# A decoder layer's input projection by Strassen's scheme, with its weight sums on VectorE and GpSimd

## The reference

```python
z = jnp.einsum("bsd,de->bse", h, w_in) + b_in
glu_val, glu_gate, gate_c, q, k, v, f_logit, gate_a = _split_columns(z)
y_conv = _conformer_conv(glu_val, glu_gate, w_dw, b_dw, g_cn, b_cn)
y_conv = y_conv * jax.nn.silu(gate_c)
y_attn = _forgetting_attention(q, k, v, f_logit)
y_attn = y_attn * jax.nn.silu(gate_a)
y = jnp.concatenate([y_conv, y_attn], axis=-1)
sub = jnp.einsum("bse,ed->bsd", y, w_out) + b_out
h = _layer_norm(DN_ALPHA * h + sub, g_post, b_post)
```

## Time and profile before

| what | value |
|---|---|
| median of 3 runs | 1765.31 us (1764.43 to 1766.93) |
| span of the profiled execution | 1763.0 us |
| TensorE busy | 1733.5 us (98%) |
| VectorE busy | 1071.8 us (61%) |
| ScalarE busy | 539.6 us (31%) |
| GpSimd busy | 215.4 us (12%) |
| transfers | 178.09 MB, 101 GB/s over the span |

### The profile page before, as it was taken

The page is one execution under the profiler, slowest core; times in us unless marked ns, Lnnn a source line. Parts: engine busy times, 40 slices in busy tenths (PEclk is TensorE's granted clock), DMA queues, the critical chain, the costliest instruction groups (busy, mean ns, idle before and its releaser), DMA issues. The chain is left out here.

```text
span 1763.0 us, 21898 instructions
## 1 busy us (share of the span) xinstructions
PE 1733.5 (98%) x7644; PEld 1400.0 (79%) x7644; DVE 1071.8 (61%) x1669; ACT 539.6 (31%) x791; POOL 215.4 (12%) x176
## 2 busy tenths in 40 slices
PE   7999999999999999999999999999999999999997
PEld 5888888888888888888888888888688877788885
DVE  4356757667586575765857657577754565344347
ACT  4323223222232232223223232232544432222240
POOL 0120101201012010110111101100200044000000
PEclk8999999999999999999999999999999999999999
DMA  5333342333323433333333333333233333332232
GB/s 157 109 110 87 95 110 71 110 97 94 100 73 108 105 91 96 77 104 110 95 92 77 108 100 95 98 83 86 70 108 96 119 131 132 124 115 95 95 120 96
DMA packets 259691, 178.09 MB, mean 101 GB/s; under 512 B 8193, under 2 KB 246945, under 8 KB 258737
## 3 DMA queue, kind: packets, MB, share of 16 engines
q1 hardware_dynamic: 258656, 170.39, 33.6%
q0 software_dynamic: 1008, 7.34, 1.2%
HBM read 173.48 MB, written 4.23 MB: 101 GB/s over the span
## 5 line engine op out<-in xcount | busy, mean ns | idle before, releaser
L635 PE MATMUL ps<-xh,wh 128*128 128x512 f32 x1792 | 716.4, 400 | 0.7 <-DVE wl L876 0.7
L636 PE MATMUL ps<-xl,wh 128*128 128x512 f32 x1792 | 711.9, 397 | 0.0
L637 PE MATMUL ps<-xh,wl 128*128 128x512 f32 x1792 | 711.5, 397 | 0.0
L876 DVE TENSOR_TENSOR wl<-raw,wh 128x1024 fp32r<-128x1024 f32 x280 | 370.3, 1324 | 391.0 <-ACT wh L388 387.1
L635 PEld LDWEIGHTS ps<-xh,wh 128*128 128x128 f32 x1792 | 338.8, 189 | 81.5 <-DVE wl L876 0.8
L637 PEld LDWEIGHTS ps<-xh,wl 128*128 128x128 f32 x1792 | 338.4, 189 | 81.8
L636 PEld LDWEIGHTS ps<-xl,wh 128*128 128x128 f32 x1792 | 338.9, 189 | 80.1 <-issue 0.5
L388 ACT ACTIVATE wh<-raw 128x1024 fp32r<-128x1024 f32 x280 | 288.2, 1054 | 297.0 <-PE ps L637 221.8
L921 DVE SCALAR_TENSOR_TENSOR y<-u,taps,y 128x512 f32 (+1 forms) x240 | 193.6, 807 | 0.0
L921 DVE SCALAR_TENSOR_TENSOR odd<-u,taps,odd 128x512 f32<-128x512 f32 x224 | 186.6, 833 | 0.0
L635 PE MATMUL ps<-wh,yh 128*128 128x512 f32 x464 | 183.0, 394 | 3.1 <-DVE yl L1162 3.1
(11 more groups left out here) (167 smaller groups left out, 1068.3 us busy)
## 6 DMA issues: line engine op xcount, KB each, us to landing
raw<-in_w_in_dram SPq DMA_DIRECT2D x224, 512.0 KB, 3.7
raw<-in_w_out_dram SPq DMA_DIRECT2D x64, 512.0 KB, 3.6
probs<-forget_sums_dram SPq DMA_DIRECT2D x16, 256.0 KB, 7.4
res<-in_x_dram POOLq DMA_DIRECT2D x4, 1024.0 KB, 5.3
out_dram<-res SPq DMA_DIRECT2D x8, 512.0 KB, 2.7
probs<-forget_sums_dram SPq DMA_DIRECT2D x16, 192.0 KB, 6.2
probs<-forget_sums_dram SPq DMA_DIRECT2D x16, 128.0 KB, 4.8
y<-in_x_dram SPq DMA_DIRECT2D x2, 768.0 KB, 9.0
```

Of the source, the lines that this page charges most:

```text
L635: nc.tensor.matmul(o, ah, bh, start=start, stop=False, skip_group_check=True)
L636: nc.tensor.matmul(o, ah, bl, start=False, stop=False, skip_group_check=True)
L637: return nc.tensor.matmul(o, al, bh, start=False, stop=True, skip_group_check=True)
L876: vec.tensor_tensor(wl[:, 2 * par + h, :], raw[:, h, :], wh[:, 2 * par + h, :], ALU.subtract) \
```

## The change

The input projection is made by Strassen's scheme (Winograd's form) over blocks of two by two. A *group* g is two tiles of weights (128 columns each) by the two halves of the 2048 rows, and its four blocks (B11, B12, B22, B21; 1024 rows by 128 columns each, 512 KB) are loaded into a ring of seven slots in `raw`. The tokens are the other two halves (256 each). In place of eight block products there are seven, called units, each of 8 x 3 matmuls of 128 by 128 by 256. There are 56 groups (48 for the heads, then 8 for `gate_c`) and 392 units.

- Four sums of weight blocks a group: `sum_1` and `sum_2` on VectorE, `sum_3` and `sum_4` on GpSimd, each of 128 by 1024, in `raw`. The sums of the input's blocks are made once at the start (`x_sums`), and the input is kept as seven factors (`xh`, `xl` of 7 x 8 x 256).
- Each unit has its own weights to split: 392 `high` and `low` of 1024 columns (224 before).
- Products are added up in PSUM where the scheme allows it, and otherwise by small instructions: three copies on ScalarE (`p1`, `p5`, `nu1`) and five on VectorE (`c12`, `c22`, `c21`, `c11`, `s57`) a group, all of 256 columns.
- The seven factors of the input take the room of `y`: the attention's output, the convolution's output and the gates go to DRAM as they are made and are loaded again, for the norm's mean and variance and for the output projection.
- The convolution has one accumulator, in PSUM (bank `CONV`), where it had two in SBUF. Its taps are spread over the slots by `TAPS_AT`.
- The bias of a head is loaded as before, but only the mask is added (by GpSimd), not the row's own cumulated sum. The probabilities are scaled on ScalarE, not on VectorE.
- All loops are written out; there is no loop on the chip.

A group has seven slots of time. In slot s TensorE makes one unit, ScalarE the `high` of the unit two later and VectorE its `low`; `slot_unit` and `ORDER` say which. The product with number 4 of a group is made in slot 2 of the next. The groups of a head are of three kinds, by `g % 3`: the first (0) makes q and k, and beside it runs the attention's product with v of the head before (`ptl`, `values`); the second (1) makes v and the attention's gate, and `kl`, `ql` and `scores` of this head stand there; the third (2) makes value and gate, with the maxima, the exponentials and the turning of v and the probabilities.

```diff
-BODY_KINDS = (Q, K, V, GATE_A, VAL, GLU)
-BODY_TAPS = (7, 7, 7, 6, 5, 0)
...
+ORDER = (1, 2, 4, 5, 6, 7, 3)
+FACTOR = {1: 0, 2: 1, 4: 2, 5: 3, 6: 4, 7: 5, 3: 6}
+HEAD_GROUPS = 3 * HEADS
+GROUPS = HEAD_GROUPS + HEADS // 2
+UNITS = 7 * GROUPS
+RING = 7
+B11, B12, B22, B21, SUM = range(5)
+SOURCE = {1: B11, 2: B21, 3: B22, 4: SUM, 5: SUM, 6: SUM, 7: B12}
+SLOTS = 3
...
+TAPS_AT = ((1, 0, 1, 2, 1, 2, 2), (2, 1, 1, 2, 2, 2, 2), (0, 1, 2, 2, 2, 2, 1))
...
+            def loads(g):
+
+                if g >= 2:
+                    sp.wait_ge(t4_done, g - 1)
+                load_block(g, B11, 0, 0)
+                if g >= 2:
+                    sp.wait_ge(low_done, at(g - 2, 4) + 1)
+                load_block(g, B12, 0, 1)
+                if g >= 1:
+                    sp.wait_ge(low_done, at(g - 1, 1) + 1)
+                    sp.wait_ge(t1_done, g)
+                load_block(g, B22, 1, 1)
+                if g >= 1:
+                    sp.wait_ge(low_done, at(g - 1, 7) + 1)
+                load_block(g, B21, 1, 0)
+
...
+            def sum_3(g):
+
+                pool.wait_ge(t1_done, g + 1)
+                pool.wait_ge(block_in[B22][g % 2], parity(g))
+                o = raw[:, ring(g, B12), :]
+                nc.gpsimd.tensor_tensor(o, o, raw[:, ring(g, B22), :], ALU.add).then_inc(t3_done, 1)
+
+            def sum_4(g):
+
+                pool.wait_ge(low_done, at(g, 6) + 1)
+                pool.wait_ge(block_in[B21][g % 2], parity(g))
+                o = raw[:, ring(g, SUM), :]
+                nc.gpsimd.tensor_tensor(o, o, raw[:, ring(g, B21), :], ALU.add).then_inc(t4_done, 1)
...
+            def high(n):
...
+                if n >= 3:
+                    act.wait_ge(unit_done, n - 2)
+                nc.scalar.activation(w_high(n), source(n), ACT.Copy).then_inc(high_done, 1)
...
+            def product(n, k):
+
+                g, m = UNIT_OF[n]
+                a = slice(P * k, P * (k + 1))
+                f = FACTOR[m]
+                return mm3(ps[:, BANK_OF[m], 0:TOK], w_high(n)[:, a], w_low(n)[:, a], xh[:, f, k, :], xl[:, f, k, :],
+                           k == 0 and m in (1, 2, 5, 7))
...
+                pe.wait_ge(low_done, n + 1)
                 for k in range(HALF):
...
+            def scores(i):
+
+                pe.wait_ge(ql_done, i + 1)
+                pe.wait_ge(kl_done, i + 1)
...
+            def low(n):
+
+                dve.wait_ge(high_done, n + 1)
+                src = source(n) if n < UNITS else raw_out(n - UNITS)
+                vec.tensor_tensor(w_low(n), src, w_high(n), ALU.subtract).then_inc(low_done, 1)
...
+            def sum_1(g):
+
+                dve.wait_ge(block_in[B11][g % 2], parity(g))
+                dve.wait_ge(block_in[B12][g % 2], parity(g))
+                if g >= 1:
+                    dve.wait_ge(low_done, at(g - 1, 3) + 1)
+                else:
+                    dve.wait_ge(fw_low, 2)
+                vec.tensor_tensor(raw[:, ring(g, SUM), :], raw[:, ring(g, B11), :], raw[:, ring(g, B12), :],
+                                  ALU.add).then_inc(t1_done, 1)
+
+            def sum_2(g):
+
+                dve.wait_ge(low_done, at(g, 5) + 1)
+                dve.wait_ge(block_in[B22][g % 2], parity(g))
+                o = raw[:, ring(g, SUM), :]
+                vec.tensor_tensor(o, o, raw[:, ring(g, B22), :], ALU.add).then_inc(t2_done, 1)
...
+            def x_low(k):
+                dve.wait_ge(xh_done, k + 1)
+                vec.tensor_tensor(xl[:, :, k, :], x_tmp[k % 2][:, 1:8, :], xh[:, :, k, :], ALU.subtract).then_inc(xl_done, 1)
...
+                    if w < TAPS - 1:
+                        vec.scalar_tensor_tensor(out=o, in0=u[:, w:w + SEQ], scalar=tap, in1=o,
+                                                 op0=ALU.mult, op1=ALU.add).then_inc(tap_done, 1)
...
+                if s == 0 and g:
...
+                    vec.scalar_tensor_tensor(out=o2[:, 0:TOK], in0=nu1[:, :], scalar=bias(cols, k2, i2),
+                                             in1=ps[:, R5, 0:TOK], op0=ALU.add, op1=ALU.subtract).then_inc(c12_done, 1)
+                    vec.scalar_tensor_tensor(out=o2[:, TOK:SEQ], in0=nu1[:, :], scalar=bias(cols, k2, i2), in1=s57[:, :],
+                                             op0=ALU.add, op1=ALU.subtract).then_inc(c22_done, 1)
...
+                    vec.scalar_tensor_tensor(out=o1[:, TOK:SEQ], in0=ps[:, R7, 0:TOK], scalar=bias(cols, k1, i1),
+                                             in1=nu1[:, :], op0=ALU.add, op1=ALU.subtract).then_inc(c21_done, 1)
...
+                    vec.tensor_tensor(tile_of(g, 0)[:, 0:TOK], ps[:, R2, 0:TOK], p1[:, :], ALU.add).then_inc(c11_done, 1)
...
+                    vec.tensor_tensor(s57[:, :], ps[:, R7, 0:TOK], p5[:, :], ALU.add).then_inc(s57_done, 1)
...
+            for g in range(GROUPS):
+                for s in range(7):
+                    n = slot_unit(g, s)
+                    i, count = convs(g, s)
+                    before = 0 if g % 3 == 0 and s == 4 else count // 2
+                    conv(i, before)
+                    if n is not None:
+                        low(n + 2)
+                        if n + 2 < UNITS and UNIT_OF[n + 2][1] == 5:
+                            sum_2(UNIT_OF[n + 2][0])
+                    if s == 5 and g < GROUPS - 1:
+                        sum_1(g + 1)
+                    if g == 0 and s in (0, 3):
+                        forget(s)
+                    evict(g, s)
+                    attention(g, s)
```

More of the change, by code:

```diff
@@ new lines, in end_y, with bias @@
+        def end_y(ring_y, last, end, q):
+            return last[:, q, :] if q < 4 else ring_y[:, q % 2, :] if q < 6 else end[:, q - 6, :]
+        def bias(table, kind, i):
+            return table[:, kind * HEADS + i:kind * HEADS + i + 1]
+        x_loaded = [sem(f"x_loaded{n}") for n in range(len(X_CUTS))]
+        f_loaded, rows_loaded, fbias_loaded, dw_loaded = (sem("f_loaded"), sem("rows_loaded"), sem("fbias_loaded"),
+                                                          sem("dw_loaded"))
@@ L241, in load_bias, with load_out @@
+            def load_out(t):
+                p, q = t // PER_PASS, t % PER_PASS
+                row = D + P * q if q < HEADS else P * (q - HEADS)
+                sp.dma_start(raw_out(t), w_out[row:row + P, 1024 * p:1024 * (p + 1)]).then_inc(out_in[t % 3], 16)
             def load_bias(h):
@@ new lines, in _ @@
+            for g in range(GROUPS):
+                sum_3(g)
+                if g < HEAD_GROUPS and g % 3 == 1:
+                    masks(g // 3)
+                sum_4(g)
+                if g < HEAD_GROUPS and g % 3 == 0 and g >= 6:
+                    add_conv(g // 3 - 2)
+                if g == HEAD_GROUPS:
+                    add_conv(HEADS - 2)
+                if g == HEAD_GROUPS + 2:
+                    add_conv(HEADS - 1)
+                if HEAD_GROUPS + 3 <= g < HEAD_GROUPS + 7:
+                    for j in range(4):
+                        add_square(4 * (g - HEAD_GROUPS - 3) + j)
@@ L1038, in forget @@
+            sum_1(0)
+            low(1)
+            def forget(step):
+                if step == 0:
+                    dve.wait_ge(f_act, 1)
+                    dve.wait_ge(fbias_loaded, 16)
+                    vec.scalar_tensor_tensor(out=fz, in0=ps[0:HEADS, R5, :], scalar=fbias[:, :], in1=f_low[0:HEADS, :],
+                                             op0=ALU.add, op1=ALU.add).then_inc(f_vec, 1)
+                    return
                 dve.wait_ge(f_act, 4)
@@ L1116, in _ @@
-            for j in range(HEADS):
-                center(j)
-                if j >= 4 and j % 2 == 0:
-                    add_square(j - 3)
-                if j in (5, 7):
-                    low(t + 4, 1, (j - 5) // 2)
-                if j == 11:
-                    gate(2, 2)
-            add_square(HEADS - 3)
-            add_square(HEADS - 1)
+                vec.tensor_scalar(neg_cum[0:HEADS, :], fcum, -1.0 / SCALE, None, ALU.mult).then_inc(f_vec, 1)
+                vec.memset(csum[:, :], 0.0).then_inc(vec_const, 1)
```

1727 lines of the change are left out of this document (908 added, 819 removed).

## The result

The changed kernel takes 1928.63 us (median of 4 runs, 1927.26 to 1929.03), where the kernel before took 1764.88 us beside it: a ratio of 1.0927, with a 95% interval of 1.0912 to 1.0943. The span of the profiled execution is 1927.2 us. Forecast were 1899 us of time, 1897 us of span.

The account below looks back on a forecast made before the run. VectorE, with its locks from GpSimd's sums, was taken as the bound (chance 0.52): start 50 + first units 79 + 15 heads 1215 + last units 175 + output 378 = 1897 us span, 1899 us time; range 1785 to 1985.

Parts of the forecast that it names:

- idle time of TensorE ahead of most units, released by `low`: Sign for VectorE as the bound: TensorE idle before the first matmul of most units until VectorE's `low` is done.
- VectorE's 65 us: VectorE's work in one head, summed from undisturbed instruction times, PSUM taps priced as SBUF ones: 65 us.
- third rival: Taps in PSUM cost another 0.11 us each, or clock losses double with a fall at `values`: 1960 to 2040 us; chance 0.15.
- TensorE's 64.4 us: TensorE's time for one head: 21 units of 2.81 us, matmuls 0.117 us apart, plus 5.4 us of attention.
- second rival: TensorE stays the bound, with a head of 70.4 us and 1725 us in all, faster; chance 0.1.
- The lock, 10.4 us: Per head, VectorE instructions with two SBUF inputs held up by GpSimd's additions: 10.4 us, bounds 0 and 17.5.
- first rival: The lock costs less than half: 5 us lost, a head of 73 to 77, time 1780 to 1838 us; chance 0.2.
- The waits, 5.1 us: Per head, on top of VectorE's 75.4 us: 2.4 behind `scores`, 1.0 behind `values`, 1.7 for the lowered clock.
- The last 52 units, 175 us: Stage after the 15 heads: 175 us, where TensorE alone would need 146.
- the four with `center` some 22 each: Among the last 52 units, the four groups with `center` were put at some 22 us each.
- The output, 378 us: Output projection and end: 378 us, 3 us over the 375.1 of the kernel before.
- I cost it at 3 us: Storing y and z in DRAM and loading them again, 12 MB, for the turn into the output projection: 3 us.

Follow-up runs that it names:

- e3: Changed kernel with taps 1 to 29 of the convolution's 31 left out, for timing alone: 1777.62 us, ratio 1.0073.
- e4: Changed kernel with `ql` and the last `ptl` made earlier in their slots: 1820.39 us, ratio 1.0315.
- e1: Changed kernel with GpSimd's `sum_3` and `sum_4` cut to 2 columns, for timing alone: 1834.35 us, ratio 1.0394.
- e6: e4 with a new tap table, three or four taps behind each instruction that releases a GpSimd sum: 1776.11 us, ratio 1.0063.
- e7: Changed kernel with taps 1 to 29 taking both inputs from SBUF, still writing to PSUM, for timing alone: 2030.81 us, ratio 1.1507.
- e5: Changed kernel with `square` one slot later in gate groups and the norm ahead of `low` in output steps: 1887.06 us, ratio 1.0693.
- e8: Changed kernel with the edits of e4, e5 and e6 together: 1734.52 us, ratio 0.9829.
- e10: e8 with `sum_3` and `sum_4` moved from GpSimd to VectorE: 1856.25 us, ratio 1.0518.

## Why the prediction was right, and where it was off

- **The bound.** That VectorE takes over from TensorE was right. e3 and e4 show it: less of VectorE's work gives 9.3 us a head, and without the two waits the head is VectorE's work and locks. But one sign that the prediction named did not come: idle time of TensorE ahead of most units, released by `low`. There are four gaps a head and `low` ends none of them. VectorE's work and locks cost time because they make `ql`, `ptl` and two other results late.
- **VectorE's 65 us.** Measured 65.9. The tap into PSUM, for which there was no row, has the price of the one from SBUF, 0.66 us from start to start. The half of the third rival that had dearer taps is out.
- **TensorE's 64.4 us.** The step "I take half of 0.234" was low. In the changed kernel matmuls of 256 columns are 0.12 us apart. Between these two starts lie the 8 x 3 of a unit:

```profile
515.09 0.28 PE L836 MATMUL ps<-xh,whl 128*128 128x256 f32 x1
...
517.97 0.28 PE L836 MATMUL ps<-xh,whl 128*128 128x256 f32 x1
```

 A unit is 2.88 us, and the head's floor 66 to 67. It cost the prediction nothing, since this was not the bound, but it made the second rival too fast.
- **The lock, 10.4 us.** The mechanism was right (e1, e6, e7), the size was not: 6.3 us at most, 5.0 on `low` and 1.1 on `u` beside `csum`. The step that failed is "`kl` at once in the second (2.4)" and "`ql` is next (2.4)". Both start 0.16 us before GpSimd and are not held; the `low` behind each loses 0.76 and 0.74. And the masks, which with `csum` were counted at 2.3 us, hold up no instruction of VectorE in this head; they lie beside taps and evictions. The first rival, "less than half", is not what happened either: 6.3 lies between.
- **The waits, 5.1 us.** VectorE waits 7.2 us. That behind `scores` is 3.5 with the clock's part in it (2.4 + 1.7 predicted), and that behind `values` 2.7 (1.0 predicted): TensorE's idle time there is 3.51 us, near the 3 forecast, but the granted clock falls there too (0.74 at 524.50, in this head, and 0.50 at 683.30), which the prediction had in its third rival only; the rest, 1.0 us, are two short waits. The two errors, 4.1 us too much for locks and 2.1 too little for waits, leave 79.9 against 81.
- **The last 52 units, 175 us.** The step "the four with `center` some 22 each" was wrong. The prediction gives no terms for the 22 (and its terms for this stage add up to 173). It names no chain, and `square` stands in ScalarE's order ahead of the next `high`, a chain through two engines of 3.72 us a turn; the group takes 27.8 us. The chain is not all of it: e5, without the chain, has 24.1 us, and e1, with the chain and without GpSimd's sums, has 23.9. Measured 201.7.
- **The output, 378 us.** The step that failed is "I cost it at 3 us". With y in DRAM, the norm and the gate of the conv tiles came into the output steps, and I counted the transfers and not the instructions. It was 23.7 us more than before; e5 takes 26.3 away with no transfer changed.
- **The second rival, 1725 us.** Its threshold was that VectorE's head falls below 72. e6 has 69.9 and is still at 1776, since the two late stages, 538 us in the rival's sum, are 598 there. e8, with TensorE busy in 67.1 of a head's 69.9 us, comes nearest to what it described, and is at 1734.5.

What stays open: why a gate group of e8 is still at 24 us where TensorE needs 20.2 (7 x 2.88). `low` of up to 3.4 us stand there, beside GpSimd's sums, and e10, which has none, gains only 3 us in that stage; its group is 22.8 us.

## What to carry to other kernels

When work moves from the engine that bounds to one that had room, add up the second engine's head again with what disturbs it, and then look for the places where the bound engine waits for a single late instruction: here, moving two instructions forward was worth 7.1 us a head, where leaving out 29 taps, some 20 us of VectorE's work, was worth 9.3. Beside a GpSimd addition put VectorE's instructions that read PSUM; those with two SBUF inputs that start behind it stood still here until it ended. And where a stage has a chain that goes back and forth between two in-order engines, count one turn of the chain, not each engine's sum.
